# A PEER block on one Trainium2 core: gate products in rounded f32, u's low parts on GpSimd, three row buffers

## The chip, the cores and the metric

One of the eight cores of a Trainium2 chip is used. The metric is the device time of the whole program in microseconds, the median of several runs. TensorE (PE) multiplies matrices, with PEld for its weight loads; VectorE (DVE), ScalarE (ACT) and GpSimd (POOL) work elementwise; SyncE (SP) issues most DMAs; GpSimd issues the gathers.

## The reference, cut to what matters

A block of 512 tokens of width 1024: an mLSTM and differential-attention mixer, then a PEER layer, which this case is about. For each token and each of 8 heads, 16 of 128 x 128 experts are chosen, and a softmax over their scores gives gates:

```python
act = gelu(einsum("td,thkd->thk", hb, expert_u[eb]))
out = einsum("thk,thkd->td", act * gb, expert_v[eb])
```

Here `eb` are the chosen expert numbers and `gb` the gates. Each token so has 128 slots (8 heads of 16).

## The kernel before, in words

The mixer and the query projection take the first 844 us and are not touched. The last part is `experts_block`. It treats tokens 128 to 511 densely: every one of the 16384 experts is computed for every token, in 128 steps of 128 experts, and a gate matrix that is mostly zero picks the chosen ones. The first 128 tokens are treated sparsely, by gathering rows.

*The u stage*, 128 steps (`NEXP`). SP loads a tile of `expert_u` (512 KB) into a ring of four. ScalarE rounds it to f32r, `uhi` (L2067); VectorE subtracts to get the low part, `ulo` (L2156); TensorE does 24 products with 384 columns (hi x hi, hi x lo, lo x hi for eight slices, L1994); ScalarE takes the gelu (L2092), and SP stores the result to `act_scratch`. `uhi` and `ulo` have two buffers each. PE's step n waits for `lo_done`, the count of finished low parts; SP loads tile n when the low part n - 4 is done.

Beside these steps VectorE does other work in program order, after its `cut(n + 1)`: in steps 0 to 7 the search of the last two heads, in steps 8 to 55 the routing of four token tiles (`route`, 12 steps each), which finds the experts and gates of every slot. Steps 56 to 59 are between. Steps 60 to 107 are the gate steps (`gates`, L2285 and L2009): each builds the gate matrix for 8 tokens. VectorE compares `con.iota` with the slots' row numbers (`hot_i`) and column numbers (`hot_j`), and multiplies `hot_i` by the gates, three instructions of 128x1024 in f32; TensorE multiplies the one-hot matrices, one f32 product of 128 columns for each token, which the profile shows as two passes; ScalarE copies the result to `stage`, and SP flushes it to `gate_scratch`. The one-hot tiles have two buffers, so VectorE may be two gate steps ahead of TensorE (`g_done`). Steps 108 to 127 are called the tail here.

*The v stage*, again 128 steps. SP loads a tile of `expert_v`, the stored activations and the gates; VectorE multiplies them (`wt`, L2302) and forms two low parts (L2305, L2307); ScalarE rounds twice; TensorE does 18 products with 512 columns (L2038), accumulating over all steps.

*The gathered rows* of the first 128 tokens run beside both stages. For each of 128 slots GpSimd issues an indirect DMA that brings, for each token, one 8 KB row with its expert's u and v (`fetch`, L1780). VectorE takes the dot product with h (`dot`, L1787), ScalarE the gelu and the product with the gate (`weigh`, two small instructions), and VectorE adds coefficient times v to `acc` (`add`, L1806) one step later. There are `ROWS` buffers; the fetch of slot r waits until slot r - ROWS has been added. `slots_of_steps` says in which step the dot of each slot stands: every fourth step in the routing, each of steps 56 to 59, every second gate step, three of four in the tail (51 in all), and 77 spread evenly over the first 120 v steps.

## Time and profile before

| | us |
|---|---|
| median of 3 runs | 2015.2 (2012.47 to 2019.03) |
| span of the profiled execution | 2011.3 |
| PE busy | 1937.0 (96%) |
| DVE busy | 1489.4 (74%) |
| ACT busy | 719.0 (36%) |
| POOL busy | 481.5 (24%) |

The times of the runs are whole device times; the profiled execution is shown by its span, from the first to the last instruction, and its own time outside the span is not listed. The expert part runs from about 844 us to the end. Shares of busy time are averages over stages with different limits, so the stages are read one by one. Matmuls are pipelined: the spacing of their starts, not the duration of one, is what a product costs. The same holds for VectorE's long instructions, whose successors start before the recorded end.

### The profile page before, as it was taken

The numbers are of one execution on the slowest core, as the hardware profiler recorded it, in microseconds if no ns is written. First come the engines' busy times: TensorE is split into PE (matmuls) and PEld (weight loads), VectorE is DVE, ScalarE is ACT, GpSimd is POOL, SyncE is SP. The second block draws the span as 40 slices with busy tenths as digits, with TensorE's granted clock in tenths as the row PEclk, the third lists the DMA queues.
The fourth block names the chain that finished last, engine by engine and source line by source line (L and its number), as shares of the span: only waits on it lengthen the run. The fifth ranks groups of instructions, "written<-read, shape, count | busy, mean of one in ns | idle before, by whom it ended". The sixth has DMA issues, their size and how long they took to land.

```text
span 2011.3 us, 27895 instructions
## 1 busy us (share of the span) xinstructions
PE 1937.0 (96%) x10341; PEld 1714.5 (85%) x10341; DVE 1489.4 (74%) x2727; ACT 719.0 (36%) x1324; POOL 481.5 (24%) x240
## 2 busy tenths in 40 slices
PE   5999998999999989999999999999999999999998
PEld 3889776889877888899999999999988888888886
DVE  5677445364475545787889999997689889899895
ACT  4110234010252243344443444444444444444443
POOL 0443202343213113100111521111222323332221
PEclk9999999999999999999999999999999999999999
DMA  6335511354212422257767688888999999999993
GB/s 253 105 106 182 172 54 48 106 191 147 63 43 73 158 80 88 72 173 255 234 225 241 231 318 297 299 296 300 412 395 401 401 400 398 400 398 401 400 375 115
DMA packets 212642, 467.99 MB, mean 233 GB/s; under 512 B 13576, under 2 KB 157120, under 8 KB 193344
## 3 DMA queue, kind: packets, MB, share of 16 engines
q1 hardware_dynamic: 194112, 332.54, 47.6%
q0 software_dynamic: 18432, 134.23, 16.9%
q8 instruction: 51, 0.84, 0.2%
q14 instruction: 47, 0.39, 0.1%
HBM read 412.19 MB, written 54.53 MB: 232 GB/s over the span
## 4 chain that ended last, share of the span: by engine, by line
PE 52%; DVE 2%; DMA 2%; ACT 1%; issue 0%; POOLq 0%; POOL 0%; SPq 0%; ACTq 0%; DVEq 0%
PE xin_out L2038 26%; PE xin_ps_u L1994 22%; PE xin_out L2016 4%; DMA con_raw<-in_expert_u 2%; DVE in_ulo L2156 1%; ACT in_uhi L2067 0%; DVE experts_rows L1787 0%; DVE experts_acc L1806 0%; DVE over_s_stage L2170 0%; ACT L2109 0%; ACT over_v_vhi L2074 0%; DVE over_v_vlo L2305 0%; POOLq L95 0%; POOL xin_x L2147 0%; DVE over_s_stage L2253 0%
## 5 line engine op out<-in xcount | busy, mean ns | idle before, releaser
L1780 POOL DMA_INDIRECT experts_rows<-in_expert_rows,experts_idx x128 | 247.3, 1932 | 873.2 <-DVE experts_acc L1806 738.4
L1994 PE MATMUL xin_ps_u<-con_h_hi,in_uhi 128*128 128x384 f32 x1024 | 349.0, 341 | 9.4 <-DVE in_ulo L2156 7.2
L1994 PE MATMUL xin_ps_u<-con_h_hi,in_ulo 128*128 128x384 f32 x1024 | 343.3, 335 | 0.0
L1994 PE MATMUL xin_ps_u<-con_h_lo,in_uhi 128*128 128x384 f32 x1024 | 343.3, 335 | 0.0
L2038 PE MATMUL xin_out<-over_v_vhi,xin_whi 128*128 128x512 f32 x768 | 239.1, 390 | 2.1 <-DVE xin_wlo L2307 2.0
L2038 PE MATMUL xin_out<-over_v_vhi,xin_wlo 128*128 128x512 f32 x768 | 238.8, 390 | 0.0
L2038 PE MATMUL xin_out<-over_v_vlo,xin_whi 128*128 128x512 f32 x768 | 238.5, 390 | 0.0
L2156 DVE TENSOR_TENSOR in_ulo<-con_raw,in_uhi 128x1024 fp32r<-128x1024 f32 x127 | 155.5, 1224 | 78.3 <-ACT in_uhi L2067 75.9
L488 POOL TENSOR_TENSOR weights_wlo<-con_raw,weights_whi 128x2048 fp32r<-128x2048 f32 x32 | 147.5, 4609 | 251.9 <-DVE weights_whi L561 251.9
L1994 PEld LDWEIGHTS xin_ps_u<-con_h_hi,in_uhi 128*128 128x128 f32 x1024 | 193.1, 189 | 13.7 <-DVE in_ulo L2156 11.1
L1994 PEld LDWEIGHTS xin_ps_u<-con_h_lo,in_uhi 128*128 128x128 f32 x1024 | 193.2, 189 | 0.0
L1994 PEld LDWEIGHTS xin_ps_u<-con_h_hi,in_ulo 128*128 128x128 f32 x1024 | 192.7, 188 | 0.0
L2038 PEld LDWEIGHTS xin_out<-over_v_vhi,xin_whi 128*128 128x128 f32 x768 | 144.0, 188 | 33.4 <-DVE over_v_vlo L2305 2.7
L2074 ACT ACTIVATE over_v_vhi<-con_raw 128x1024 fp32r<-128x1024 f32 x128 | 135.0, 1055 | 103.8 <-DMA con_raw<-in_expert_v 88.6
L2092 ACT ACTIVATE in_act<-xin_ps_u 128x384 f32<-128x384 f32 x128 | 62.9, 491 | 300.2 <-PE xin_ps_u L1994 300.2
L2038 PEld LDWEIGHTS xin_out<-over_v_vhi,xin_wlo 128*128 128x128 f32 x768 | 144.3, 188 | 29.9
L2038 PEld LDWEIGHTS xin_out<-over_v_vlo,xin_whi 128*128 128x128 f32 x768 | 144.3, 188 | 29.7
L2305 DVE TENSOR_TENSOR over_v_vlo<-con_raw,over_v_vhi 128x1024 fp32r<-128x1024 f32 x128 | 156.4, 1222 | 9.1 <-ACT over_v_vhi L2074 8.8
L1806 DVE SCALAR_TENSOR_TENSOR experts_acc<-experts_rows,experts_coef,experts_acc 128x1024 f32<-128x1024 f32 x127 | 162.8, 1282 | 0.1
L1787 DVE SCALAR_TENSOR_TENSOR experts_rows<-experts_rows,con_h 128x1024 f32<-128x1024 f32 x128 | 156.3, 1221 | 0.1
L2067 ACT ACTIVATE in_uhi<-con_raw 128x1024 fp32r<-128x1024 f32 x127 | 133.9, 1054 | 9.3 <-DMA con_raw<-in_expert_u 9.0
L2076 ACT ACTIVATE xin_whi<-xin_wt 128x384 fp32r<-128x384 f32 x128 | 67.2, 525 | 177.7 <-DVE xin_wt L2302 177.2
(344 smaller groups left out, 3742.4 us busy)
## 6 DMA issues: line engine op xcount, KB each, us to landing
con_raw<-in_expert_u SPq DMA_DIRECT2D x128, 512.0 KB, 4.7
con_raw<-in_expert_v SPq DMA_DIRECT2D x128, 512.0 KB, 12.0
con_raw<-in_w_in SPq DMA_DIRECT2D x38, 1024.0 KB, 6.0
act_scratch<-in_act SPq DMA_DIRECT2D x128, 192.0 KB, 2.4
experts_hot<-act_scratch SPq DMA_DIRECT2D x128, 192.0 KB, 11.8
gate_scratch<-in_stage SPq DMA_DIRECT2D x12, 1024.0 KB, 7.1
gate_scratch<-over_s_stage SPq DMA_DIRECT2D x12, 1024.0 KB, 7.7
experts_hot<-gate_scratch SPq DMA_DIRECT2D x16, 768.0 KB, 14.1
```

Source lines behind the costliest of these rows:

```text
L488: pool.tensor_tensor(wlo[s][:], raw[s][:], as_f32(whi[s][:]), ALU.subtract).then_inc(w_lo, 1)
L1780: pool.indirect_dma_start(out=self.rows[:, r % ROWS, :], out_offset=None, in_=table, in_offset=at).then_inc(self.row_in[r % ROWS], 16)
L1787: dve.scalar_tensor_tensor(out=u, in0=u, scalar=1.0, in1=h0, op0=ALU.mult, op1=ALU.mult, accum_out=self.dots[:, r:r + 1]).then_inc(self.do ...
L1806: dve.scalar_tensor_tensor(out=self.acc[:], in0=v, scalar=self.coef[:, r:r + 1], in1=self.acc[:], op0=ALU.mult, op1=ALU.add).then_inc(self ...
L1994: mm = pe.matmul(ps_u[s % 2][:, 0:TD], a[s % 2][:, k, :], m[:, k, P:T], start=(i == 0), stop=(i == 3 * KD - 1))
L2016: mm = pe.matmul(ps_g[b][:, k, :], hot_j[q % 2][:, 4 * b + k, :], hot_i[q % 2][:, 4 * b + k, :], start=True, stop=True)
L2038: product = lambda s, t, h, w, m, **flags: pe.matmul(out[t][h][:], w[s][:, t * P:(t + 1) * P], m[s][:, h * 512:(h + 1) * 512], **flags)
L2067: act.activation(uhi[n % 2][:], cut_of[n % U_RING], ACT.Copy).then_inc(hi_done, 1)
L2074: act.activation(vhi[s][:], v[s], ACT.Copy).then_inc(vhi_done, 1)
L2076: act.activation(whi[s][:], wt[n % 2][:], ACT.Copy).then_inc(whi_done, 1)
L2156: dve.tensor_tensor(ulo[n % 2][:], cut_of[n % U_RING], as_f32(uhi[n % 2][:]), ALU.subtract).then_inc(lo_done, 1)
L2305: dve.tensor_tensor(vlo[s][:], v[s], as_f32(vhi[s][:]), ALU.subtract).then_inc(vlo_done, 1)
```

## The change

Four things are changed together.

1. *Low parts of u.* From tile 25 on (`POOL_CUTS`) GpSimd does the subtraction that gives `ulo`, the same instruction as VectorE's. In GpSimd's program it stands before the row fetches of that step. VectorE keeps tiles up to 24.
2. *Gates in rounded f32.* `hot_i` and `hot_j` are now f32r. The gate is split into a rounded part (`g_hi`) and the rest (`slot[2]`), and a third one-hot tile `hot_l` carries the rest. VectorE does four 128x1024 instructions a gate step in place of three; TensorE does two f32r products for a token, accumulating, in place of one f32 product.
3. *Three row buffers* in place of four (`ROWS`); the query tile `qry` gets its own place in the memory that the later tiles reuse.
4. *Slots spread anew:* every second step of the routing (16 slots), each of steps 56 to 59, every sixth gate step (8), each step of the tail (20): 48, and 80 over the first 120 v steps.

```diff
--- before.py
+++ after.py
@@ -1576,7 +1576,7 @@
 TD = T - P
 ND = TD // P
 SLOTS = PH * TOPK
-ROWS = 4
+ROWS = 3
 NEXP = NK
 
 
@@ -1766,6 +1766,7 @@
 
     def __init__(self, al):
         self.rows = al.sb("rows", [P, ROWS, 2 * D])
+        self.hot_lo = al.sb("hot_lo", [P, 2 * G_TOK * NK], F32R)
         self.acc = al.sb("acc", [P, D])
         self.idx = al.sb("idx", [P, SLOTS], U32)
         self.gate, self.dots, self.raw, self.coef = [al.sb(n, [P, SLOTS]) for n in ("gate0", "dots", "raw", "coef")]
@@ -1818,13 +1819,16 @@
 FIRST_LOADS = N_HOT0 + N_HOT + 14
 
 
+POOL_CUTS = range(N_SEARCH + R_STEPS + 5, NEXP)
+
+
 def slots_of_steps():
 
 
     inside = [[] for n in range(NEXP)]
     r = 0
     for n in range(N_SEARCH + R_STEPS + 4, NEXP):
-        if (n < N_ROUTE and n % 4 == 0) or N_ROUTE <= n < N_HOT0 or (N_HOT0 <= n < N_HOT0 + N_HOT and n % 2 == 0) or (n >= N_HOT0 + N_HOT and n % 4 != 3):
+        if (n < N_ROUTE and n % 2 == 0) or N_ROUTE <= n < N_HOT0 or (N_HOT0 <= n < N_HOT0 + N_HOT and n % 6 == 0) or n >= N_HOT0 + N_HOT:
             inside[n].append(r)
             r += 1
     outside = [[] for n in range(NEXP)]
@@ -1844,14 +1848,14 @@
 G_RUN = 4 * 8 * G_TOK
 
 
-def experts_block(nc, con, ring, hot, hot_all, stage, early, got, rt, A, hT, acts, gmat, x1, dst, vhi, vlo, cut_hi, cut_lo):
+def experts_block(nc, con, ring, hot_r, hot_all, stage, early, got, rt, A, hT, acts, gmat, x1, dst, vhi, vlo, cut_hi, cut_lo):
 
 
     u = A["expert_u"]
     with Alloc(nc, "xin") as al:
         raw, landed = ring.tile, ring.u_in
         cut_of = [x.rearrange("p (k n) -> p k n", k=KD) for x in raw]
-        uhi, ulo, act_t, slot, gsum, ginv = early
+        uhi, ulo, act_t, slot, g_hi, gsum, ginv = early
 
 
         spare, taken = stage[1][:].rearrange("p a b -> p (a b)"), [0]
@@ -1873,7 +1877,9 @@
         gate0 = got.gate[:].rearrange("p (h k) -> p h k", h=PH)
         flat = lambda ap: ap.rearrange("p h k -> p (h k)")
 
-        hot_j, hot_i = hot[0:2], hot[2:4]
+        steps_of = lambda ap: [x.rearrange("p (t n) -> p t n", n=NK) for x in (ap[:, i * G_TOK * NK:(i + 1) * G_TOK * NK]
+                                                                             for i in range(ap.shape[1] // (G_TOK * NK)))]
+        hot_j, hot_i, hot_l = steps_of(hot_r)[0:2], steps_of(hot_r)[2:4], steps_of(got.hot_lo[:])
         ps_u = [al.ps(f"ps_u{i}", [P, 512]) for i in range(2)]
         out = [[al.ps(f"out{t}{h}", [P, 512]) for h in range(2)] for t in range(ND)]
         ps_g = [out[ND - 1][b][:].rearrange("p (k n) -> p k n", n=NK) for b in range(2)]
@@ -1905,7 +1911,7 @@
         block = al.block()
         assert N_TAIL > 0 and N_TAIL % 4 == 0
         STAGES, RANKS = 10, 9
-        closed, summed = al.sem("closed"), al.sem("summed")
+        closed, summed, g_cut = al.sem("closed"), al.sem("summed"), al.sem("g_cut")
 
         @block.sync
         def _(sp):
@@ -2013,8 +2019,9 @@
 
                     wait(pe, staged, 2 * m + b - 1)
                     for k in range(4):
-                        mm = pe.matmul(ps_g[b][:, k, :], hot_j[q % 2][:, 4 * b + k, :], hot_i[q % 2][:, 4 * b + k, :],
-                                       start=True, stop=True)
+                        for i, part in enumerate((hot_i, hot_l)):
+                            mm = pe.matmul(ps_g[b][:, k, :], hot_j[q % 2][:, 4 * b + k, :], part[q % 2][:, 4 * b + k, :],
+                                           start=(i == 0), stop=(i == 1))
                     mm.then_inc(g_done, 1)
 
             for n in range(N_HOT0):
@@ -2127,11 +2134,26 @@
 
         @block.gpsimd
         def _(pool):
+            def cut(n):
+
+                if n == POOL_CUTS[0]:
+                    pool.wait_ge(lo_done, n)
+                pool.wait_ge(hi_done, n + 1)
+                pool.tensor_tensor(ulo[n % 2][:], cut_of[n % U_RING], as_f32(uhi[n % 2][:]), ALU.subtract).then_inc(lo_done, 1)
+
             pool.wait_ge(got.idx_done, 1)
-            for r in range(ROWS):
+            r = ROWS
+            for i in range(ROWS):
+                got.fetch(pool, i, A["expert_rows"])
+            for n in range(NEXP):
+                if n + 1 in POOL_CUTS:
+                    cut(n + 1)
+                for added in IN_AT[n - 2] if n > 1 else []:
+                    got.fetch(pool, r, A["expert_rows"])
+                    r += 1
+            while r < SLOTS:
                 got.fetch(pool, r, A["expert_rows"])
-            for r in range(ROWS, SLOTS):
-                got.fetch(pool, r, A["expert_rows"])
+                r += 1
             pool.wait_ge(ms0_done, 1)
             pool.tensor_tensor(rstd0[:], ms0[:], con.pow_half[:, 0:1], ALU.pow).then_inc(pow0_done, 1)
             def power(t):
@@ -2278,20 +2300,26 @@
 
             def copy_slots(tt):
                 dve.wait_ge(slots_t, tt)
-                for i in range(3):
-                    op = dve.tensor_copy(slot[i][:, (tt - 1) * P:tt * P], ps_g[0][:, i, :])
-                op.then_inc(slots_done, 1)
+                cols = slice((tt - 1) * P, tt * P)
+                dve.tensor_copy(g_hi[:, cols], ps_g[0][:, 2, :]).then_inc(g_cut, 1)
+                for i in range(2):
+                    dve.tensor_copy(slot[i][:, cols], ps_g[0][:, i, :])
+                dve.wait_ge(g_cut, tt)
+                dve.tensor_tensor(slot[2][:, cols], ps_g[0][:, 2, :], as_f32(g_hi[:, cols]),
+                                  ALU.subtract).then_inc(slots_done, 1)
 
             def gates(m):
 
                 wait(dve, g_done, 2 * (m - 1))
                 shape = [P, G_TOK, NK]
                 keys = con.iota[:].unsqueeze(1).to_broadcast(shape)
-                i_s, j_s, g_s = [slot[x][:, m * G_TOK:(m + 1) * G_TOK].unsqueeze(2).to_broadcast(shape) for x in range(3)]
-                dve.tensor_tensor(hot_i[m % 2], keys, i_s, ALU.is_equal).then_inc(is_row, 1)
+                i_s, j_s, gl_s, gh_s = [x[:, m * G_TOK:(m + 1) * G_TOK].unsqueeze(2).to_broadcast(shape)
+                                        for x in (slot[0], slot[1], slot[2], as_f32(g_hi))]
+                dve.tensor_tensor(hot_l[m % 2], keys, i_s, ALU.is_equal).then_inc(is_row, 1)
                 dve.tensor_tensor(hot_j[m % 2], keys, j_s, ALU.is_equal)
                 dve.wait_ge(is_row, m + 1)
-                dve.tensor_tensor(hot_i[m % 2], hot_i[m % 2], g_s, ALU.mult).then_inc(hot_done, 1)
+                dve.tensor_tensor(hot_i[m % 2], as_f32(hot_l[m % 2]), gh_s, ALU.mult)
+                dve.tensor_tensor(hot_l[m % 2], as_f32(hot_l[m % 2]), gl_s, ALU.mult).then_inc(hot_done, 1)
 
             def weighted(n):
                 s = n % RING
@@ -2316,7 +2344,7 @@
                     dve.wait_ge(slots_done, ND)
                 if N_HOT0 <= n < N_HOT0 + N_HOT:
                     gates(n - N_HOT0)
-                if n < NEXP - 1:
+                if n < NEXP - 1 and n + 1 not in POOL_CUTS:
                     cut(n + 1)
                 if n < N_SEARCH:
                     rt.search(dve, PH - LATE_HEADS + n // PIECES, n % PIECES)
@@ -2379,22 +2407,28 @@
         vhi, vlo = [[av.sb(f"{n}{i}", [P, D], F32R) for i in range(RING)] for n in ("vhi", "vlo")]
     with Alloc(nc, "experts") as al:
         al.sb("rounded", [P, 8 * D])
+        with Alloc(nc, "over_h") as ah:
+
+            hot_r = ah.sb("hot_r", [P, 4 * G_TOK * NK], F32R)[:]
         cut_hi, cut_lo = al.sem("cut_hi"), al.sem("cut_lo")
         hot_all = al.sb("hot", [P, 4 * G_TOK * NK])[:]
         hot = [hot_all[:, i * G_TOK * NK:(i + 1) * G_TOK * NK].rearrange("p (t n) -> p t n", n=NK) for i in range(4)]
+        with Alloc(nc, "over_q") as aq:
+
+            qry = aq.sb("qry", [P, HC, T])
         got = Gathered(al)
         with Alloc(nc, "in") as ai:
 
             stage = [ai.sb("stage0", [P, NK, 8 * G_TOK])]
             rt = Routing(al, stage[0][:])
             uhi, ulo = [[ai.sb(f"{n}{i}", [P, KD, P], F32R) for i in range(2)] for n in ("uhi", "ulo")]
-            qry = got.rows[:].rearrange("p a n -> p (a n)").rearrange("p (c t) -> p c t", t=T)
             query_block(nc, con, slots, ring, A, hT, qry, hot[0:2], rt, uhi, ulo, cut_hi, cut_lo, begun)
             stage.append(stage1)
             act_t, slot = [[ai.sb(f"{n}{i}", [P, TD]) for i in range(c)] for n, c in (("act", 4), ("slot", 3))]
+            g_hi = ai.sb("g_hi", [P, TD], F32R)
             gsum, ginv = ai.sb("gsum", [P, PH]), ai.sb("ginv", [P, PH])
-            early = uhi, ulo, act_t, slot, gsum, ginv
-        experts_block(nc, con, ring, hot, hot_all, stage, early, got, rt, A, hT, acts, gmat, x1, out, vhi, vlo, cut_hi,
+            early = uhi, ulo, act_t, slot, g_hi, gsum, ginv
+        experts_block(nc, con, ring, hot_r, hot_all, stage, early, got, rt, A, hT, acts, gmat, x1, out, vhi, vlo, cut_hi,
                       cut_lo)
```

## Rows read from the trace of the kernel before

**Rows 1.** The page: its first line and the busy line of section 1.

```profile
span 2011.3 us, 27895 instructions
...
PE 1937.0 (96%) x10341; PEld 1714.5 (85%) x10341; DVE 1489.4 (74%) x2727; ACT 719.0 (36%) x1324; POOL 481.5 (24%) x240
```

**Rows 2.** Windows: bounds, length; PE, PEld, DVE, ACT, POOL busy; clock; DMA; GB/s.

```profile
948.00:1086.00 138.00, 134.03 (x762) 131.09 (x761) 124.80 (x281) 56.42 (x87) 13.42 (x8) 1.00 0.70 228
1086.00:1103.00 17.00, 16.12 (x95) 15.85 (x93) 13.74 (x18) 7.27 (x15) 4.52 (x3) 1.00 0.80 266
1103.00:1389.00 286.00, 285.61 (x1919) 285.29 (x1920) 279.14 (x267) 134.63 (x241) 64.40 (x26) 1.00 0.81 286
1389.00:1479.00 90.00, 85.98 (x485) 85.02 (x484) 59.51 (x67) 37.46 (x74) 20.52 (x14) 0.98 1.03 403
...
1600.00:1700.00 100.00, 99.87 (x440) 82.13 (x439) 88.12 (x121) 43.27 (x81) 29.41 (x16) 1.00 1.03 401
```

**Rows 3.** The chain that ended last: start us, us, what.

```profile
1107.79 1.78 PE xin_out L2016 x16
1109.57 4.17 PE xin_ps_u L1994 x24
...
1683.51 302.22 PE xin_out L2038 x1332
```

**Rows 4.** Timeline of GpSimd and VectorE at two places: start us, us, instruction.

```profile
141.63 4.65 POOL L488 TENSOR_TENSOR weights_wlo<-con_raw,weights_whi 128x2048 fp32r<-128x2048 f32 x1 [6.26 <-DVE weights_whi L561]
141.85 4.72 DVE L138 SCALAR_TENSOR_TENSOR proj_m_ada_acc<-proj_m_ada_w,con_silu_c,proj_m_ada_acc 128x256 f32<-128x256 f32 x1
...
767.84 4.61 POOL L1676 TENSOR_TENSOR weights_wlo<-con_raw,weights_whi 128x2048 fp32r<-128x2048 f32 x1 [8.40 <-ACT weights_whi L1738]
771.02 0.28 DVE L1624 MATCH_REPLACE8 in_stage<-in_stage 128x128 f32<-128x128 f32 x1
```

**Rows 5.** Timeline in the gate steps: a fetch, and VectorE's work beside it.

```profile
1116.32 6.22 POOL L1780 DMA_INDIRECT experts_rows<-in_expert_rows,experts_idx  x1 [5.21 <-DVE experts_acc L1806]
...
1120.50 1.22 DVE L1787 SCALAR_TENSOR_TENSOR experts_rows<-experts_rows,con_h 128x1024 f32<-128x1024 f32 x1
1121.65 1.22 DVE L2291 TENSOR_TENSOR experts_hot<-con_iota,in_slot 128x1024 f32<-128x1024 f32 x1
1122.78 1.22 DVE L2292 TENSOR_TENSOR experts_hot<-con_iota,in_slot 128x1024 f32<-128x1024 f32 x1
...
1126.19 1.28 DVE L1806 SCALAR_TENSOR_TENSOR experts_acc<-experts_rows,experts_coef,experts_acc 128x1024 f32<-128x1024 f32 x1
1127.38 1.23 DVE L2291 TENSOR_TENSOR experts_hot<-con_iota,in_slot 128x1024 f32<-128x1024 f32 x1
```

**Rows 6.** Groups by line and shape: count, busy us, mean ns, idle before.

```profile
L1780 POOL DMA_INDIRECT experts_rows<-in_expert_rows,experts_idx x128 | 247.3, 1932 | 873.2 <-DVE experts_acc L1806 738.4 <-DVE experts_idx L2244 106.4 <-DVE experts_acc L1803 23.3
L488 POOL TENSOR_TENSOR weights_wlo<-con_raw,weights_whi 128x2048 fp32r<-128x2048 f32 x32 | 147.5, 4609 | 251.9 <-DVE weights_whi L561 251.9
L2067 ACT ACTIVATE in_uhi<-con_raw 128x1024 fp32r<-128x1024 f32 x127 | 133.9, 1054 | 9.3 <-DMA con_raw<-in_expert_u 9.0 <-PEq L95 0.3
L2092 ACT ACTIVATE in_act<-xin_ps_u 128x384 f32<-128x384 f32 x128 | 62.9, 491 | 300.2 <-PE xin_ps_u L1994 300.2
L1795 ACT ACTIVATE experts_coef<-experts_raw,experts_gate 128x1 f32<-128x1 f32 x128 | 37.8, 295 | 4.1
L138 DVE SCALAR_TENSOR_TENSOR proj_d_ada_acc<-proj_d_ada_w,con_silu_c,proj_d_ada_acc 128x256 f32<-128x256 f32 x56 | 27.2, 485 | 2.0
L2233 DVE TENSOR_TENSOR over_s_stage<-over_s_stage 128x2048 f32<-128x2048 f32 x8 | 18.3, 2285 | 0.0
```

**Rows 7.** Timeline of the weight loads: four passes, their moving operand one column.

```profile
21.86 0.52 PEld L264 LDWEIGHTS head_ps_ada<-con_ones,head_acc 128*128 128x128 f32 x4 [0.73 <-DVE head_acc L138]
```

**Rows 8.** The fetches: landing over all of them; then those of 1389 to 1479 us.

```profile
DMA to landing us min/median/max: 5.7/9.2/14.3
...
experts_rows<-in_expert_rows,experts_idx POOLq DMA_INDIRECT x14, 9.2
```

## The prediction

> **What bounds the kernel now.** I read the page first, then the windows by stage, then single instructions. TensorE is busy 96% of the span [rows 1], and in the expert part the chain that ends last runs through its products: those of u (L1994), of the gates (L2016) and of v (L2038) [rows 3]. The windows cut the expert part into the stages that the change touches [rows 2]: steps 24 to 55 with the routing (948 to 1086 us), steps 56 to 59 (to 1103), the 48 gate steps (to 1389), the 20 steps of the tail (to 1479), and the v stage. In the gate steps TensorE is never idle (285.6 of 286.0 us): a step is 24 u products in 4.17 us and 16 gate passes in 1.78 [rows 3], 5.95 in all. VectorE is close behind it, at 279 of 286. In the tail the DMA share is 1.03 at 403 GB/s and TensorE has 4 us idle: the transfers bound it. In the v stage TensorE bounds, with the DMA engines at 401 GB/s and VectorE at 88% [rows 2].
>
> **A price that the change needs first: GpSimd beside VectorE.** At 141.63 us GpSimd begins a subtraction of two SBUF tensors, 4.65 us long; at 141.85 VectorE begins a scalar_tensor_tensor with two SBUF inputs, of a kind whose 56 instances in the other projection take 0.485 us in the mean [rows 6]. This one takes 4.72 us and ends 0.3 us after GpSimd's [rows 4].  Instructions with one input are not held: at 771 us a MATCH_REPLACE takes its 0.28 us in the middle of a subtraction [rows 4]. It works the other way as well: while VectorE issues two-input instructions back to back, a fetch of GpSimd takes 6.22 us, where their mean is 1.93 (247.3 us for 128) [rows 5, 6]. So I treat a GpSimd subtraction and a two-input VectorE instruction as exclusive. The Trainium skill (SBUF — State Buffer, "Who interferes with whom") says the same: whoever issues first has the shared ports for the whole instruction, and a VectorE instruction with two SBUF inputs contends with a GpSimd one that reads SBUF. The trace agrees, by the 4.72 us.
>
> **Part 1: u's low parts on GpSimd, steps 25 to 127.** VectorE loses 103 instructions at 1.135 us from start to start [rows 5]. GpSimd gains them. Its subtraction takes 4.609 us for 2048 elements, half of which is 2.3; with a fixed part I take 2.4 us for 1024. ScalarE's high part (1.05 us) and then 2.4 on GpSimd [rows 6] take 3.5 of the 4.17 us of a u step, so alone it would be hidden, with 0.6 us to spare.
>
> **Part 2: the gate steps.** VectorE now does four 128x1024 instructions (two comparisons, two multiplications), all with two SBUF inputs: 4 x 1.135 = 4.54 us. A slot in every sixth step costs a dot and an add, 1.15 + 1.19 = 2.34 [rows 5], or 0.39 a step. Together 4.93, down from 5.73 before (4 x 1.135 and half of 2.34), so without the lock VectorE would be well clear of TensorE. With it, GpSimd's 2.4 us add to the same resource: 7.33, and about 0.1 for the two hand-overs, 7.4 us a step. Both are needed in each step: PE's next u products wait for GpSimd, and its gate products for VectorE, which can be at most two gate steps ahead. Nothing gets this below the sum. 48 x 7.4 = 355 us against 286: **+69**. Ends: 7.25 without hand-overs (+62), and 7.8 if the queues line up badly (+88).
>
> TensorE in these steps: 16 f32 passes become 16 rounded products of 128 columns. No rounded product that narrow is in the trace. Rounded products of 384 columns come every 0.173 us and of 512 every 0.227 [rows 3], 0.054 for 128 columns, so the straight line gives 0.067 at 128. But each needs its own weight load, and four f32 passes with a moving operand of one column lie at (0.52 - 0.19) / 3 = 0.110 us [rows 7]: there only the load can set the pace. I take 0.111, what a pass costs now: no gain. Ends: 0.067 and 0.222 (what an f32 product with both of its passes costs). All but the last lie under the 7.4: 4.17 + 1.78 = 5.95. The Trainium skill (TensorE: Matmul & The Clock Gate, "Back-to-back issue gap") has about 81 ns for streams of such pairs at 128 columns. By that the PE step would be 5.5, and the sum is unchanged, since PE isn't the bound.
>
> **Part 3: the routing, steps 25 to 55.** VectorE loses 1.135 a step and gains a slot in every second step where it had one in four (8 more, 2.34 each). Twelve steps hold one token tile. Two-input work in them: 6 slots 14.0, four products of pick (L2226, L2233) at 2.28, 9 in all [rows 6], small ones about 3, together 26; GpSimd 12 x 2.4 = 29. That is 55 us of exclusive work where twelve steps take 50 now at 4.17, and it comes in bursts, with 0.6 us of slack for each cut. Against it: 4 us of TensorE's idle now (138 - 134) go, being waits for cuts. I take +0.5 us a step for 31 steps, **+15**; ends 0 and +27. Steps 56 to 59 have a slot each: 2.34 + 2.4 + a fetch that also reads SBUF, 5.4 against 4.25: **+5** (2 to 8). The longer copy of the slots, two more small instructions before step 60, is 0.5 us and inside this.
>
> **Part 4: the tail, 20 slots in place of 15 and three row buffers.** A row fetch is 128 rows of 8 KB, 1.05 MB. Of the 15 slots 14 were fetched in these 90 us [rows 8]; now about 20. The stage moved 90 x 403 = 36.3 MB; with 6.3 MB more at the same rate it is 105.7 us: +16. The new buffers give a second bound. Slot r+3 is fetched when slot r is added. Round that loop: landing 9.2 us [rows 8], dot 1.2, ScalarE's two small steps 0.5 (one is 0.295), gelu 0.5, high part 1.05 [rows 6], GpSimd's cut 2.4 (the fetch is queued behind the cut, and the next cut behind the fetch), 0.3 of semaphores: 15.2 us for 3 slots, 5.1 a step; with one hold by the lock, 17.5 or 5.8. I take 5.5 x 20 = 110 against 90: **+20** (10 to 30).
>
> **Part 5: the v stage.** No cuts there, so no lock but for fetches. 80 slots in place of 77: 3 x 1.05 MB at 401 GB/s = 8 us if it is DMA-bound, 0 if TensorE hides it (VectorE's 3 x 2.34 us lie in its 12% idle). A slot comes every 1.5 steps of 4.09 us; from add to dot of the third next are 3.5 steps, 14 us, against 9.2 of landing (max. 14.3) [rows 8]. I take **+3** (0 to +8).
>
> **Sum.** 69 + 15 + 5 + 20 + 3 = 112 us. The profiled execution's span is 2011.3 us [rows 1]; its own total isn't given apart from the runs, whose median 2015.2 lies 3.9 above the span. 2011.3 + 112 = 2123 of span, **2127 us** with the same 3.9.
>
> **Rivals.**
> (a) *TensorE's narrow rounded products run at 0.222.* For: nothing rounded in the trace is under 256 columns. Against: from 512 to 384 columns the cost falls in proportion, to 0.173, and at 128 it would stand above both. The gate step is 4.17 + 16 x 0.222 = 7.7, TensorE is the bound just above the lock, +84 instead of +69: 2142. It decides from 0.20 us a product.
> (b) *The lock doesn't hold for these instructions* (the 4.72 us was one case). Gate steps then stay at 5.95: 0; routing -4, since the waits for cuts go; +1, +14 and +3 for the rest: 2029.
> (c) *The other side: as (b), and the rounded products cost 0.067.* A gate step is 4.17 + 1.07 = 5.24, VectorE's 4.93 beneath it: 48 x 5.24 = 251, -35. With -4, +1, +14, +3: 1994. It decides if loads hide below 0.11 and, above all, if VectorE's port is free: with the lock the 7.4 stays whatever TensorE saves. For it: the load bound is an f32 row. Against: rows 4 and 5.
> (d) *GpSimd starves for whole bursts of VectorE* (as in the 6.22 us), and each cut that is late holds gelu, the row fetch behind it and the next cut. Routing and tail both take their upper ends: 2127 + 12 + 10 = 2149. Against: TensorE's wait soon empties VectorE's queue too.
>
> **Chances.** Forecast 0.68, (a) 0.08, (b) 0.08, (c) 0.04, (d) 0.12. Runs of this kernel lie within 0.3% of each other (6 us), which is what can be told from no change. Faster only in (c): 0.04; same 0.01; slower 0.95. Range: parts' ends give 2015 + 62 + 0 + 2 + 10 + 0 = 2089 to 2015 + 88 + 27 + 8 + 30 + 8 = 2176, which all at once is unlikely above; I widen below for a lock that costs less than whole instructions: 2072 to 2165, leaving out (b) and (c).
>
> **What would show it.** Gate steps of 7.3 to 7.5 us with TensorE idle between steps, waiting for GpSimd's L2156-like subtraction; VectorE's 128x1024 instructions with a mean well over 1.22 us, single ones near 3.5 (held for the 2.4). Rounded gate products at 0.11 apart. The tail at 105 to 115 us with waits of the dots for rows. Wrong: gate steps of 5.9 with VectorE's durations unchanged (b), or under 5.5 (c).

## The result, and the profile after

The changed kernel takes **2141.2 us** (median of four runs, 2137.9 to 2141.5), the kernel before 2014.2 beside it: a ratio of 1.0623 [1.0607, 1.064], slower by 127 us. The forecast was 2127. The span grew from 2011.3 to 2139.7 us; the profiled execution's own time lies 1.8 us above its span, not 3.9.

The page after (its first line, the busy line, and the shares of the chain that ended last by engine), against [rows 1]:

```profile
span 2139.7 us, 27947 instructions
...
PE 1984.6 (93%) x10341; PEld 1740.1 (81%) x10341; DVE 1626.6 (76%) x2675; ACT 718.9 (34%) x1324; POOL 755.3 (35%) x343
...
DVE 24%; PE 19%; DMA 10%; issue 3%; POOL 2%; ACT 1%; SPq 1%; POOLq 0%; DVEq 0%; ACTq 0%
```

VectorE has 52 instructions fewer and is busy 137 us longer. The windows of the stages, with the columns of [rows 2] (the routing, one token tile of it, the gate steps, the tail, 100 us of the v stage):

```profile
950.80:1119.40 168.60, 143.53 (x759) 136.61 (x760) 165.15 (x253) 57.33 (x101) 116.84 (x47) 0.96 0.67 225
1001.00:1067.00 66.00, 55.67 (x293) 53.08 (x292) 64.41 (x114) 22.68 (x40) 44.94 (x18) 0.95 0.68 227
...
1137.40:1484.90 347.50, 308.69 (x1909) 300.51 (x1908) 345.59 (x225) 128.94 (x208) 165.39 (x60) 0.95 0.59 193
1484.90:1596.30 111.40, 93.45 (x497) 88.78 (x495) 73.76 (x58) 38.53 (x81) 80.66 (x38) 0.95 0.96 352
1700.00:1800.00 100.00, 100.00 (x442) 82.36 (x441) 87.14 (x121) 41.93 (x79) 26.83 (x16) 1.00 1.04 402
```

In the routing and in the gate steps TensorE now idles and VectorE doesn't. Before it was the other way round. In the tail the DMA engines are a little less full (0.96 and 352 GB/s, were 1.03 and 403), TensorE is idle for 18 us, and the stage is longer. Only the v stage looks as it did.

For the comparisons I cut every trace at the same places, the starts of ScalarE's gelu of steps 24, 55, 59, 107 and 127 (L2092 before, L2099 after), so that a stage is the same steps in all of them (the routing is 31 of them, 25 to 55). The stages and the span are those of one profiled execution, and the median is that of all runs: the profiled one lay 7.7 us under its median in e3, and 5.8 and 5.3 above it in e8 and e12.

| kernel | routing, 25-55 | 56-59 | gate steps | tail | v stage | span | median | ratio [95%] |
|---|---|---|---|---|---|---|---|---|
| before | 136.0 | 16.6 | 285.8 | 90.2 | 533.5 | 2011.3 | 2014 to 2016 | |
| after | 168.6 | 18.0 | 347.5 | 111.4 | 543.4 | 2139.7 | 2141.2 | 1.0623 [1.0607, 1.064] |
| e1, no cuts on GpSimd | 142.6 | 18.0 | 294.4 | 99.9 | 540.7 | 2046.8 | 2048.8 | 1.0163 [1.0146, 1.018] |
| e2, only the cuts | 151.6 | 18.2 | 326.0 | 94.7 | 533.1 | 2072.6 | 2076.7 | 1.0305 [1.0288, 1.0323] |
| e3, GpSimd only writes | 139.8 | 17.2 | 325.7 | 104.1 | 541.9 | 2077.3 | 2086.8 | 1.0366 [1.0335, 1.0396] |
| e4, slots and rows | 142.5 | 17.9 | 285.8 | 99.0 | 542.3 | 2038.6 | 2039.2 | 1.0118 [1.0093, 1.0144] |
| e5, three rows | 136.0 | 16.6 | 285.8 | 90.3 | 533.8 | 2013.1 | 2015.1 | 1.0001 [0.9992, 1.001] |
| e6, slots | 142.5 | 17.9 | 285.8 | 96.5 | 542.2 | 2034.1 | 2037.0 | 1.0118 [1.0102, 1.0133] |
| e7, bf16 one-hots | 136.0 | 16.6 | 383.1 | 93.7 | 534.0 | 2116.6 | 2118.1 | 1.0512 [1.0497, 1.0527] |
| e8, cuts in 11 steps | 139.8 | 16.7 | 285.8 | 94.6 | 537.4 | 2023.3 | 2019.3 | 1.0027 [1.0013, 1.004] |
| e9, e3 without slots in gate steps | 145.9 | 19.1 | 297.0 | 106.5 | 542.1 | 2060.9 | one run | |
| e10, rounded gates alone | 136.0 | 16.6 | 328.9 | 94.9 | 533.8 | 2060.9 | 2062.3 | 1.023 [1.0203, 1.0257] |
| e11, tail's slots to v | 136.0 | 16.6 | 285.8 | 94.4 | 538.1 | 2019.8 | 2020.4 | 1.0022 [1.0008, 1.0035] |
| e12, tail's slots to gates | 136.0 | 16.6 | 286.3 | 93.5 | 534.3 | 2020.0 | 2016.5 | 1.0005 [0.9991, 1.0019] |

After against before, in span: +32.6 routing, +1.4, +61.7 gate steps, +21.2 tail, +9.9 v stage, +1.6 ahead of the gelu of step 24: 128.4.

Two gate steps of the kernel after, VectorE's timeline, against [rows 5]:

```profile
1298.47 3.40 DVE L2318 TENSOR_TENSOR experts_hot_lo<-con_iota,in_slot 128x1024 fp32r<-128x1024 f32 x1
1301.80 1.21 DVE L2319 TENSOR_TENSOR over_h_hot_r<-con_iota,in_slot 128x1024 fp32r<-128x1024 f32 x1
...
1305.20 1.21 DVE L2318 TENSOR_TENSOR experts_hot_lo<-con_iota,in_slot 128x1024 fp32r<-128x1024 f32 x1
1306.34 3.41 DVE L2319 TENSOR_TENSOR over_h_hot_r<-con_iota,in_slot 128x1024 fp32r<-128x1024 f32 x1
```

and GpSimd's beside it:

```profile
1297.86 2.93 POOL L2142 TENSOR_TENSOR in_ulo<-con_raw,in_uhi 128x1024 fp32r<-128x1024 f32 x1 [3.02 <-ACT in_uhi L2074]
1305.34 3.32 POOL L2142 TENSOR_TENSOR in_ulo<-con_raw,in_uhi 128x1024 fp32r<-128x1024 f32 x1 [4.55 <-ACT in_uhi L2074]
```

Here a VectorE instruction takes 1.21 us or 3.41: it is held for 2.20 us, once for each subtraction. Of its 211 long instructions in the gate steps, 163 take 1.2 to 1.3 us, 46 take 3.4 and two lie between (2.47 and 2.65). The subtraction at 1305.34 began while VectorE was in an instruction, took 3.32, and ended as that hold did, at 1308.7. The groups of the whole trace say which instructions are held:

```profile
L2142 POOL TENSOR_TENSOR in_ulo<-con_raw,in_uhi 128x1024 fp32r<-128x1024 f32 x103 | 299.1, 2905 | 263.6 <-ACT in_uhi L2074 263.2
L2322 DVE TENSOR_TENSOR experts_hot_lo<-experts_hot_lo,in_slot 128x1024 fp32r<-128x1024 f32 x48 | 108.7, 2264 | 0.0
L2255 DVE TENSOR_TENSOR over_s_stage<-over_s_stage 128x2048 f32<-128x2048 f32 x8 | 26.9, 3369 | 0.0
L2263 DVE TENSOR_REDUCE over_s_stage<-over_s_stage 128x128 f32<-128x2048 f32 x8 | 18.2, 2274 | 0.0
```

The product over 2048 elements rose from 2285 ns [rows 6] to 3369; the sum over as many, with one input, stayed (2277 ns in e1). The Trainium skill (SBUF — State Buffer, "Who interferes with whom") has GpSimd's reads contend with a VectorE instruction of two SBUF inputs, and adds that `tensor_scalar` can enter modes that take both ports as well. The trace agrees with both: in the routing the three small shifts of L2275 (`tensor_scalar`, 128 columns) take 2.69 us together beside a subtraction, and the nine of the routing 1189 ns each in the mean, where e1 (below) has 221.

TensorE waits for what the lock delays. The largest waits of its products (total us, times, longest):

```profile
PE xin_ps_u L2000 <- POOL in_ulo L2142: 43.3, 29, 3.2
PE xin_out L2023 <- DVE experts_hot_lo L2322: 32.9, 21, 2.8
```

### The profile page after: what moved, and what is told of

The parts are those of the page before. It is cut to its first block, busy times and chain, and to the rows that moved or that the text cites. A ratio compares the mean times of both kernels' runs of the same rounds, so it can differ in the third digit from the quotient of the medians.

```text
span 2139.7 us, 27947 instructions
## 1 busy us (share of the span) xinstructions
PE 1984.6 (93%) x10341; PEld 1740.1 (81%) x10341; DVE 1626.6 (76%) x2675; ACT 718.9 (34%) x1324; POOL 755.3 (35%) x343
## 4 chain that ended last, share of the span: by engine, by line
DVE 24%; PE 19%; DMA 10%; issue 3%; POOL 2%; ACT 1%; SPq 1%; POOLq 0%; DVEq 0%; ACTq 0%
PE xin_out L2045 12%; PE xin_ps_u L2000 6%; DMA experts_hot<-act_scratch 6%; DVE experts_hot_lo L2322 5%; DVE experts_hot_lo L2318 4%; DVE over_h_hot_r L2321 2%; DVE experts_acc L1807 2%; DMA experts_rows<-in_expert_rows,experts_idx 2%; DVE over_h_hot_r L2319 2%; POOL in_ulo L2142 2%; DVE experts_rows L1788 2%; DVE over_v_vlo L2333 1%; DVE over_s_stage L2248 1%; DVE over_s_stage L2255 1%; DMA con_raw<-in_expert_v 1%
## 5 line engine op out<-in xcount | busy, mean ns | idle before, releaser
L2000 PE MATMUL xin_ps_u<-con_h_hi,in_uhi 128*128 128x384 f32 x1024 | 361.2, 353 | 48.5 <-POOL in_ulo L2142 43.3
L2142 POOL TENSOR_TENSOR in_ulo<-con_raw,in_uhi 128x1024 fp32r<-128x1024 f32 x103 | 299.1, 2905 | 263.6 <-ACT in_uhi L2074 263.2
L1781 POOL DMA_INDIRECT experts_rows<-in_expert_rows,experts_idx x128 | 221.9, 1734 | 474.4 <-DVE experts_acc L1807 357.1
L2000 PE MATMUL xin_ps_u<-con_h_lo,in_uhi 128*128 128x384 f32 x1024 | 353.4, 345 | 0.0
L2000 PE MATMUL xin_ps_u<-con_h_hi,in_ulo 128*128 128x384 f32 x1024 | 352.8, 344 | 0.0
L2000 PEld LDWEIGHTS xin_ps_u<-con_h_hi,in_uhi 128*128 128x128 f32 x1024 | 200.8, 196 | 61.5 <-POOL in_ulo L2142 49.9
L1807 DVE SCALAR_TENSOR_TENSOR experts_acc<-experts_rows,experts_coef,experts_acc 128x1024 f32<-128x1024 f32 x127 | 197.2, 1553 | 21.7 <-ACT experts_coef L1796 21.6
L2000 PEld LDWEIGHTS xin_ps_u<-con_h_lo,in_uhi 128*128 128x128 f32 x1024 | 200.8, 196 | 0.0
L2000 PEld LDWEIGHTS xin_ps_u<-con_h_hi,in_ulo 128*128 128x128 f32 x1024 | 200.5, 196 | 0.0
L1788 DVE SCALAR_TENSOR_TENSOR experts_rows<-experts_rows,con_h 128x1024 f32<-128x1024 f32 x128 | 184.2, 1439 | 18.4 <-DMA experts_rows<-in_expert_rows,experts_idx 18.0
L2099 ACT ACTIVATE in_act<-xin_ps_u 128x384 f32<-128x384 f32 x128 | 62.6, 489 | 290.1 <-PE xin_ps_u L2000 289.7
```

The source lines that it names most:

```text
L1781: pool.indirect_dma_start(out=self.rows[:, r % ROWS, :], out_offset=None, in_=table, in_offset=at).then_inc(self.row_in[r % ROWS], 16)
L1788: dve.scalar_tensor_tensor(out=u, in0=u, scalar=1.0, in1=h0, op0=ALU.mult, op1=ALU.mult, accum_out=self.dots[:, r:r + 1]).then_inc(self.do ...
L1807: dve.scalar_tensor_tensor(out=self.acc[:], in0=v, scalar=self.coef[:, r:r + 1], in1=self.acc[:], op0=ALU.mult, op1=ALU.add).then_inc(self ...
L2000: mm = pe.matmul(ps_u[s % 2][:, 0:TD], a[s % 2][:, k, :], m[:, k, P:T], start=(i == 0), stop=(i == 3 * KD - 1))
L2142: pool.tensor_tensor(ulo[n % 2][:], cut_of[n % U_RING], as_f32(uhi[n % 2][:]), ALU.subtract).then_inc(lo_done, 1)
```

## The experiments

**Cuts back on VectorE (e1), and the cuts alone (e2).** e1 is the kernel after, e2 the kernel before with GpSimd's new loop.

```diff
 e1, from after
-POOL_CUTS = range(N_SEARCH + R_STEPS + 5, NEXP)
+POOL_CUTS = range(0)
 e2, from before
+POOL_CUTS = range(N_SEARCH + R_STEPS + 5, NEXP)
...
-                if n < NEXP - 1:
+                if n < NEXP - 1 and n + 1 not in POOL_CUTS:
                     cut(n + 1)
...  (and cut(n + 1) before the fetches of each step in GpSimd's program)
```

> The changed kernel with part 1 undone: VectorE makes all low parts of u, GpSimd only fetches. Lock theory (a GpSimd subtraction and a VectorE instruction with two SBUF inputs exclude each other): what is left of the change is VectorE-bound gate steps at 4 x 1.135 + 1.135 + 0.39 = 6.07 us (+6 over 48 steps against before), +5 in the routing for 8 more slots, +15 in the tail, +10 in the v stage: 2050 us, 90 below the changed kernel. VectorE's 128x1024 instructions are back at 1.21 us, none at 3.4. Rival, that the spread of slots and the three row buffers are the main cost: above 2100 us.

> The kernel before with part 1 alone: GpSimd makes the low parts from tile 25, gates in f32 with three VectorE instructions, four row buffers, slots where they were. Lock theory: a gate step is the sum on the shared resource, 3 x 1.135 + 1.17 + 2.20 = 6.78 us, so 48 x 6.78 = 325 against 286, +39; routing three slots a tile instead of six, so 66 - 7 = 59 us a tile or 4.9 a step, +16; tail +5; in all 2077 us. Rival, no exclusion: VectorE is relieved of 1.135 us a step, gate steps stay at TensorE's 5.95, the waits of the routing go: 2007 us.

The cuts on GpSimd cost 92 us of the 127: without them 2048.8. On the kernel before they cost 61. With them or without, a gate step is the sum of VectorE's starts (1.135 us each) and, where GpSimd subtracts, 2.20 for the hold. e1, five instructions and a slot in every sixth step: 5.68 + 0.39 = 6.07; measured 6.07 in its steady part, 294.4 / 48 = 6.13 in the mean. e2, three instructions and a slot in every second: 3.40 + 1.17 + 2.20 = 6.77; measured 6.79. After: 4.54 + 0.39 + 2.20 = 7.13; measured 7.13 (42.8 us for six) from about the twelfth gate step on, 7.24 over all 48. The lock is shown.

**GpSimd only writes (e3).** Three fills take the place of the subtraction, together about as long (0.96 + 0.53 + 0.96 us). The low part of u is left out: it is zero.

```diff
-                pool.tensor_tensor(ulo[n % 2][:], cut_of[n % U_RING], as_f32(uhi[n % 2][:]), ALU.subtract).then_inc(lo_done, 1)
+                pool.memset(as_f32(ulo[n % 2][:]), 0.0).then_inc(pool_step, 1)
...  (a wait for it)
+                pool.memset(as_f32(ulo[n % 2][:, 0:KD // 2]), 0.0).then_inc(pool_step, 1)
...  (a wait for it)
+                pool.memset(as_f32(ulo[n % 2][:]), 0.0).then_inc(lo_done, 1)
```

> The changed kernel with GpSimd's subtraction replaced by three fills of the same tile (1024, 512 and 1024 elements, about 2.2 us together), so GpSimd works as long but reads no SBUF; the low part of u is left out of the result (zeros). If it is the second read that excludes, VectorE's durations are 1.21 us again, gate steps are TensorE's 4.17 + 1.75 = 5.92, routing falls to 4.2 a step, tail and v stage keep +15 and +10: 2032 us. If any GpSimd instruction holds VectorE, gate steps stay near 7.1 and the time near 2140.

This missed: 2086.8, and gate steps of 6.79. GpSimd in a gate step of e3:

```profile
1251.09 0.96 POOL L2147 MEMSET in_ulo<- 128x1024 f32 x1
1252.20 7.45 POOL L1781 DMA_INDIRECT experts_rows<-in_expert_rows,experts_idx  x1 [0.15 <-issue]
1259.64 0.98 POOL L2143 MEMSET in_ulo<- 128x1024 f32 x1
```

and VectorE beside it:

```profile
1250.80 1.22 DVE L2324 TENSOR_TENSOR over_h_hot_r<-con_iota,in_slot 128x1024 fp32r<-128x1024 f32 x1
...
1257.61 1.23 DVE L2327 TENSOR_TENSOR experts_hot_lo<-experts_hot_lo,in_slot 128x1024 fp32r<-128x1024 f32 x1
1259.81 1.23 DVE L2323 TENSOR_TENSOR experts_hot_lo<-con_iota,in_slot 128x1024 fp32r<-128x1024 f32 x1 [0.97 <-PE xin_out L2023]
```

In the gate steps the fills hold nobody: none of VectorE's 211 long instructions takes over 1.3 us. But the fetch issued at 1252.20 stays open for 7.45 us while VectorE issues without a gap, and ends when VectorE pauses for TensorE at 1258.8. The next low part is queued behind it, and TensorE waits for that. It is the mechanism of rival (d), with a fetch in the place of a subtraction. It is the whole excess of the stage: eight fetches are open for 7.45 us and more, and only the eight steps with them and the first gate step are longer than TensorE's 5.96, by 39.8 us together. Why the fetch makes no headway there, no run shows.

In the routing, VectorE's small instructions with one input are held by a fill. The cast of L2216 takes 1.10 us beside one, and 0.28 in e1 (L2211), where GpSimd only fetches:

```profile
979.07 1.10 DVE L2216 CAST over_s_stage<-in_stage 128x256 f32<-128x256 uint32 x1
979.07 0.95 POOL L2147 MEMSET in_ulo<- 128x1024 f32 x1
```

Two `tensor_scalar` of 128 columns (L2292, L2293) likewise take 1098 and 1022 ns in the mean, and 227 and 219 in e1. The dots, the adds and the products over 2048 elements, with two inputs, are not held (1.22, 1.28 and 2.28 us). All this costs little: the routing takes 139.8 us, where the kernel after, with as many slots and GpSimd about as long at work, takes 168.6.

**No slots in the gate steps (e9).** If the fetch is the cause, e3 without fetches there must be bound by TensorE. The eight slots go to the routing; the fetches that follow the slots just ahead of step 60 still fall into the first gate steps.

```diff
 from e3
-        if (n < N_ROUTE and n % 2 == 0) or N_ROUTE <= n < N_HOT0 or (N_HOT0 <= n < N_HOT0 + N_HOT and n % 6 == 0) or n >= N_HOT0 + N_HOT:
+        if (n < N_ROUTE and (n % 2 == 0 or n >= 40)) or N_ROUTE <= n < N_HOT0 or n >= N_HOT0 + N_HOT:
```

> As the run in which GpSimd only fills (low part of u left out), with the 8 slots of the gate steps moved to the routing, so that no row fetch stands in GpSimd's queue between two fills there. Its gate steps took 6.79 us on average though no VectorE instruction was held. Theory: a fetch that reads its indices from SBUF starves behind VectorE's back-to-back two-input instructions (7.45 us and up to 13.6), and the fill behind it holds TensorE: without fetches the gate steps take TensorE's 5.92 us, 284 us for 48. Rival, that the fills themselves are late or compete: 6.5 us and more. The routing gets longer by up to 15 us, which is not the question.

The chain of e9 in its gate steps:

```profile
1149.97 1.74 PE xin_out L2023 x16
1151.71 4.22 PE xin_ps_u L2000 x24
```

5.96 a step, TensorE's own sum. The stage's 297.0 is 11 us above 48 of them, all of it in the first and the fourth gate step, 11.4 us each. Fetches stand in the chain of both: the first waits for a row that lands at 1117.97, whose dot is ahead of the copy of the slots, and the fourth for a fetch that is once more open for long:

```profile
1110.01 7.96 DMA experts_rows<-in_expert_rows,experts_idx
...
1132.71 7.63 POOL experts_rows L1781
```

So GpSimd's fills cost the gate steps nothing. A subtraction does, and so does a fetch with a low part queued behind it. In the kernel before a fetch is open for 6.22 us as well [rows 5], but no low part is behind it and the steps stay at 5.95.

**Slots and rows (e4), rows (e5), slots (e6).**

```diff
 e4 and e5, from before
-ROWS = 4
+ROWS = 3
 e4 and e6, from before
-        if (n < N_ROUTE and n % 4 == 0) or ... (N_HOT0 <= n < N_HOT0 + N_HOT and n % 2 == 0) or (n >= N_HOT0 + N_HOT and n % 4 != 3):
+        if (n < N_ROUTE and n % 2 == 0) or ... (N_HOT0 <= n < N_HOT0 + N_HOT and n % 6 == 0) or n >= N_HOT0 + N_HOT:
```

(In e4 and e5 the query tile also has its own place, as after, and an unused tile fills the room of the fourth buffer.)

> The kernel before with parts 3 and 4 alone: three row buffers and the new spread of slots. The tail is bound by transfers: 6.3 MB more at 403 GB/s, +15; routing +5 (VectorE has 7 us more a tile); gate steps unchanged at TensorE's 5.95; v stage +10 as in the changed kernel: 2044 us. Rival, that the tail and v losses of the changed kernel come from GpSimd's cuts (lock, fetches queued behind cuts): here the tail stays at 90 to 95 us and the time is below 2022.

> The kernel before with three row buffers and nothing else (slots as before). The v stage lost 9.9 us in the changed kernel and as much with slots and rows together. Theory A, it is the three more row fetches (3.1 MB at 401 GB/s = 8 us): here the v stage is unchanged and the time within 3 us of before. Theory B, it is the missing buffer (14 us from add to the dot of the third next slot, against landings of 9.2 median and 14.3 at most): VectorE's dots wait for rows and the time is 5 to 10 us above before.

> The kernel before with the new spread of slots and four row buffers. Theory A (bytes): tail +8, routing +6, steps 56 to 59 +1, v stage +8 to 10: 2038 us, as with slots and rows together. Theory B (buffer): v stage at most +3, 2030 us.

Three buffers alone cost nothing (1.0001). The new slots cost 22 us: 6.5 in the routing, 1.3 after it, 6.3 in the tail, 8.7 in the v stage, and the gate steps, which they relieve, don't gain, since TensorE bounds them. With three buffers the tail has 2.5 more, within what tails differ by without any change to their work (below). The routing's 6.5 is VectorE's: it was busy 46.7 us in 52,

```profile
1000.00:1052.00 52.00, 50.49 (x289) 49.50 (x289) 46.71 (x115) 21.06 (x33) 5.03 (x3) 1.00 0.69 226
```

(a window of the kernel before, columns as in [rows 2]), and three more slots a tile make 46.7 + 3 x 2.34 = 53.7, or 4.48 a step: 31 x 4.48 = 139, measured 142.5, of which VectorE was busy for 138.3. It was 122.8 of 136.0 before.

**Rounded gates alone (e10).** e1 with the slots of before.

> The kernel before with part 2 alone: gates in rounded f32 and a high and a low part (three row buffers, which its tile needs and which cost nothing by themselves), slots and low parts as before. VectorE needs 4 x 1.135 + 1.135 + 1.17 = 6.85 us a gate step, TensorE 5.92: +43 over 48 steps, 2058 us. Rival, that the rounded products relieve TensorE enough to pay for it: under 2015 us.

2062.3. VectorE makes five instructions (5.68) and half a slot (1.17), 6.85 a step; measured 328.9 / 48 = 6.85. The fourth 128x1024 instruction, beside the cut, makes VectorE the bound of the stage, 43 us longer. With e2's 61 and e6's 22 the three edits cost 61 + 47 + 22 = 130 apart and 127 together.

**Products in bf16 (e7).** The kernel before with one-hots in bf16 (exact), built for each token by `tensor_scalar` with two operations, so that no instruction reads two tiles; the gate is in two parts.

```diff
-                dve.tensor_tensor(hot_i[m % 2], keys, i_s, ALU.is_equal).then_inc(is_row, 1)
...
+                for t in range(G_TOK):
...  (the token's numbers and gate)
+                    dve.tensor_scalar(hot_j[m % 2][:, t, :], con.iota[:], j_s, None, ALU.is_equal)
+                    dve.tensor_scalar(hot_i[m % 2][:, t, :], con.iota[:], i_s, g_s, ALU.is_equal, ALU.mult)
+                    op = dve.tensor_scalar(hot_l[m % 2][:, t, :], con.iota[:], i_s, gl_s, ALU.is_equal, ALU.mult)
```

> The kernel before with the gate step written another way: one-hot tiles in bfloat16, gates in a bfloat16 high part and the rest rounded to bfloat16, each tile made by 8 tensor_scalar instructions of 128 columns (compare with the token's number, times its gate), 24 small one-input instructions a gate step in place of three of 1024 columns; TensorE does two bfloat16 products for a token. The rounded f32 products of the changed kernel came every 0.109 us, the pace of an f32 weight load (0.110). If that load sets the pace, two-byte weights load faster and 16 products cost 16 x 0.07 to 0.08: a gate step of TensorE is 4.17 + 1.2 = 5.4 us, and at 0.13 to 0.16 us for each small instruction VectorE needs 3.1 to 3.8 + 1.135 + 1.17 = 5.4 to 6.1. Time 1988 to 2014 us. Rival: the pace of 128 columns is the same whatever the type, or a small instruction costs 0.25 us: VectorE at 8.3 a step, slower than before by over 50 us.

TensorE's side worked, 16 products in 1.06 us where the f32 passes take 1.78 [rows 3]. The first line is TensorE's timeline, the others groups of 1150 to 1400 us:

```profile
1258.50 1.06 PE L2023 MATMUL xin_out<-experts_hot 128*128 128x128 bf16 x16 [2.50 <-DVE experts_hot L2303]
```

```profile
L2302 DVE TENSOR_SCALAR experts_hot<-con_iota,in_slot 128x128 bf16<-128x128 f32 x253 | 86.6, 342 | 0.0
...
L2301 DVE TENSOR_SCALAR experts_hot<-con_iota,in_slot 128x128 bf16<-128x128 f32 x252 | 69.6, 276 | 0.0
```

VectorE's side didn't: from start to start a token takes 0.26 + 0.26 + 0.20 us, and I had expected 0.13 to 0.16 an instruction, with 0.25 as the rival. With the cut and half a slot that is 5.68 + 1.135 + 1.17 = 7.98 a step; measured 7.98.

**Cuts only beside one-input work (e8).** e2 with GpSimd's cuts in eleven steps of the routing, where VectorE searches; where the two engines take turns, each waits for the other's last low part.

```diff
-POOL_CUTS = range(N_SEARCH + R_STEPS + 5, NEXP)
+POOL_CUTS = [25] + list(range(33, 38)) + list(range(45, 50))
```

> The kernel before with GpSimd making only 11 low parts, those of routing steps in which VectorE sorts with one-input instructions (MAX8, FIND_INDEX8, MATCH_REPLACE8) in token tiles 2 and 3. If only two-input work excludes GpSimd, VectorE loses 11 x 1.135 = 12 us of work and is held only by the few dots and adds there: routing 1 to 5 us shorter than the 136 of before, 2010 to 2015 us. If the exclusion is general, routing is 11 x 1.1 = 12 us longer, 2027 us.

No gain: 1.0027, +3.8 us in the routing. The chain there:

```profile
1035.49 1.06 ACT in_uhi L2070
1036.69 2.87 POOL in_ulo L2137
1039.61 4.46 PE xin_ps_u L1997 x24
```

ScalarE's high part and GpSimd's cut in series, 4.1 us with the hand-overs, are as long as a u step, so here they stand in TensorE's chain. The holds are few, as expected: beside the eleven cuts four dots and adds are 0.8 to 1.2 us longer than alone, and the FIND_INDEX8 beside the cut at 1040.85 take 0.21 and 0.22 us as ever.

**Fewer slots in the tail (e11, e12).** If transfers bound the tail, taking three of its 15 slots away must shorten it: e11 gives them to the v stage, e12 to the gate steps, where VectorE has room. e12 was the candidate for a version faster than before.

```diff
 e11, e12
-        if ... or (n >= N_HOT0 + N_HOT and n % 4 != 3):
+        if ... or (n >= N_HOT0 + N_HOT and n % 5 in (0, 2, 4)):
 e12
-        if ... or (N_HOT0 <= n < N_HOT0 + N_HOT and n % 2 == 0) or ...
+        if ... or (N_HOT0 <= n < N_HOT0 + N_HOT and (n % 2 == 0 or n in (67, 83, 99))) or ...
```

> The kernel before with three slots moved from the tail (12 of 20 steps) to the v stage (80). If both stages go by bytes, the tail gains 3.1 MB at 403 GB/s but not below TensorE's 83.4 us and the stall after the last flush, -4 to -7, and the v stage loses 8 as in all kernels with 80 slots there: 2016 to 2019 us. If the v stage's loss came from the tail before it (a smaller lead), it stays at 533 us and the time is 2009.

> The kernel before with three slots moved from the tail, where transfers bound, to the gate steps, where VectorE has 0.22 us a step to spare (10 us, three slots take 7): tail -5, gate steps unchanged at 5.95, 2009 to 2011 us, faster than before by about 0.25%. Rival: a gate step with a dot and an add has VectorE at 6.9 us, its lead of two steps does not level that out, +3 in the gate steps, no change in all.

Neither is faster (1.0022, 1.0005): e12's 2016.5, beside 2015.4 for the kernel before, is clear of the 2009 to 2011 expected. In the profiled executions the tail didn't shorten, 94.4 and 93.5 against 90.2, though e12's was a long one, with 4.0 of its 5.3 us over the median ahead of step 24, which the edit doesn't touch. The longest transfers of the tail's chain before,

```profile
1424.31 13.26 DMA con_raw<-in_expert_u
1457.82 12.83 DMA con_raw<-in_expert_u
```

stand in e12 too:

```profile
1417.99 14.27 DMA con_raw<-in_expert_u
1458.79 11.72 DMA con_raw<-in_expert_u
```

In both, single u tiles that land late stand in the chain; the stage isn't set by its bytes alone. e7 and e10, whose tails hold the same work as before, also show 93.7 and 94.9, so some 4 us of the tail's length come and go without any change to its work; one trace of each kernel can't tell whether the steps ahead of it or the execution decides. No version here beats the kernel before.

## Why the prediction was right, and where it wasn't

**The gate steps: right in mechanism.** Forecast +69 (62 to 88), measured +61.7, at the lower end. That end was 7.25 us, said to be the sum without hand-overs, but 4.93 + 2.4 is 7.33, or +66. (Likewise the 5.73 of before is 4.54 + 1.17 = 5.71.) The step is the sum of VectorE's starts and one hold. It came out at 7.13 for the 7.4 because the hold is 2.20, not 2.4, and no hand-over is added to it. "Nothing gets this below the sum" held to 0.02 us in e2, e10 and the kernel after.

**The rounded product: right.** The kernel after, in its chain:

```profile
1472.99 1.74 PE xin_out L2023 x16
1474.72 4.22 PE xin_ps_u L2000 x24
```

16 products in 1.74 us are 0.109 each, the weight load's pace (0.110 was forecast from [rows 7]). Rival (a) falls, and with it (c)'s 0.067. In bf16 the pace is (1.06 - 0.22) / 15 = 0.056, so the 0.109 goes with the 4-byte operands. The Trainium skill (TensorE: Matmul & The Clock Gate, "Back-to-back issue gap") has 81 ns for streams of such pairs; the trace lies above that in rounded f32 and below it in bf16.

**The routing: mis-sized.** Forecast +15 with an end of +27, measured +32.6: the step that failed is "in all 55 us of exclusive work where twelve steps take 50". I took as exclusive only VectorE's two-input work and GpSimd's subtractions, and let VectorE's one-input work lie beside the subtractions. (The 50 was short too: twelve of the 31 steps in 136.0 us are 52.6.) A tile takes 66.0 us, from one cut in the chain to its like:

```profile
1001.35 3.14 POOL in_ulo L2142
...
1067.36 3.13 POOL in_ulo L2142
```

VectorE's whole content of a tile is 46.7 before, less 12 cuts (13.6), plus three slots (7.0): 40.1 us. With 12 holds of 2.20 it is 66.5. Without the slots (e2) it is 59.5, and there a tile takes 58.7. The holds can be counted in VectorE's busy time. e1 has the same slots and VectorE's own cuts:

```profile
951.20:1093.70 142.50, 137.02 (x750) 128.92 (x750) 138.48 (x303) 58.15 (x101) 24.69 (x15) 1.00 0.77 263
```

Less 31 cuts (35.2) that is 103.3 us, where the kernel after has 165.15: the 61.9 between them are 28 holds of 2.20, for 31 cuts. So nearly every cut met a VectorE instruction that it could hold, and the sum was VectorE's, not that of the pair. The sum over everything that VectorE does was there to be read from the window of before.

**Steps 56 to 59: too high,** +1.4 for +5 (2 to 8).

**The tail: right in size, half right in why.** +21.2 for +20. The transfers that I put at 105.7 us weren't the longer bound: 111.4 us at 352 GB/s are 39.2 MB, which would take 97 us at 403. The loop of the row buffers was, in parts of the chain of the tail:

```profile
1511.97 8.86 DMA experts_rows<-in_expert_rows,experts_idx
...
1520.89 3.08 issue
...
1526.02 3.26 POOL in_ulo L2142
...
1529.43 1.77 POOL experts_rows L1781
...
1531.22 2.41 POOL in_ulo L2142
...
1533.79 8.60 DMA experts_rows<-in_expert_rows,experts_idx
```

From the one issue to the other 21.8 us, in which four fetches go out: 5.45 a step where I took 5.5. The 3.08 is a held dot. The loop needs both edits: slots and rows alone have 99.0, the cuts alone 94.7, together 111.4. What sets the some 4 us by which tails with unchanged work are longer than that of before stays open.

**The v stage: mis-sized.** +9.9 for +3 (0 to 8). The term that failed is the bytes: I took 3 of their 8 us, since TensorE seemed to bound. But it and the DMA engines are both at their limit: three fetches more are 3.15 MB, 7.8 us at 402 GB/s. With 80 slots there, the kernel after, e1, e3, e4, e6 and e9 have 540.7 to 543.4 (e11 538.1); with 77, before, e2, e5, e7, e10 and e12 have 533.1 to 534.3 (e8 537.4). e11 and e8 lie between the two groups, so a few us of this stage vary without its slots. In e6's first windows of the stage one sees TensorE fall behind, 220 and 231 products in 54 us where it does 240 when it isn't kept waiting, with the DMA share at 1.03 and more:

```profile
1494.10:1548.10 54.00, 51.81 (x220) 41.85 (x219) 47.20 (x65) 23.16 (x44) 13.03 (x10) 0.97 1.03 400
1548.10:1602.10 54.00, 52.50 (x231) 42.91 (x230) 48.28 (x68) 23.81 (x46) 13.94 (x9) 1.00 1.04 399
```

**The sum.** 14 us low: +17.6 routing, +6.9 v stage, +1.2 tail, +1.6 ahead of step 24, less 7.3 gate steps and 3.6 of steps 56 to 59, make 16.4 in span; 2 us of it go back, as an execution is 1.8 above its span and not 3.9. So the 14 us are what misses of +27.3 and -10.9 leave, and the total is nearer than its parts. Rival (b), no lock, is refuted by every hold. Rival (d)'s starving is there (a fetch of 7.45 us in e3, and in the kernel after a subtraction of 7.11 at 1161.96 us, after whose start VectorE still began four long instructions, so the one that issued first wasn't always served first), but the kernel after's gate steps lie only 0.11 us above the sum with the lock in the mean.

## What to carry to other kernels

Work moved to GpSimd isn't off VectorE if it reads SBUF and VectorE has instructions of two SBUF inputs in every step: add its whole time to VectorE's, all kinds of work counted, and compare that sum, stage by stage, with the engine that binds now. Look at what is queued behind an indirect DMA too: it was open for up to 13.6 us while VectorE left no gap. Where TensorE and the DMA engines were both full, three more gathers cost about their bytes (8.7 us in e6, for 7.8).
